# Sample tokens projected on the last prompt tile's mixer weights, with part of these weights kept in SBUF and a 4 KB descriptor ring

## The chip, the cores and the metric

The kernel runs on one core of one Trainium2 chip. The metric is the device time of one execution in microseconds (us), the median over runs. Lower is better. TensorE is called PE in the profile, VectorE DVE, ScalarE ACT, GpSimd POOL and SyncE SP; SP, ACT and POOL also issue DMAs.

## The reference

One layer of a decoder is computed for 512 prompt tokens (with 16 meta tokens ahead) and for 64 sample tokens (8 sequences of 8). All numbers are float32.

```python
D_MODEL = 1024; HP = 8; NK = 128; N_EXPERTS = NK * NK; DPK = 256; PEER_TOPK = 16
hp = hp + merge_heads(oa, ob, z, ...)          # ends in y @ w_out, w_out is [1024, 1024]
hp = hp + peer_ffn(rmsnorm(hp, norm2), peer_wq, peer_keys, peer_u, peer_v)

def peer_ffn block:                             # for each token
    q = (xb @ wq).reshape(-1, HP, 2, DPK // 2)
    s = einsum('thcd,hcnd->thcn', q, keys)      # scores against 2 x 128 keys for each head
    ...top 16 of each side, top 16 of the 256 sums -> 16 experts e for each of 8 heads
    h = einsum('td,thkd->thk', xb, u[e])
    w = softmax(sc) * gelu(h)
    return einsum('thk,thkd->td', w, v[e])
```

Before this come attention (group A, with a paged cache for the sample tokens) and a gated-delta recurrence (group B). Their outputs are concatenated to 1024 columns, projected by `w_out` and added to x. That projection is called the mixer in the kernel. The same steps are done for prompt and sample tokens, with the same weights. For each token 128 rows of u and v are then read (8 heads x 16 experts).

## The kernel before

The prompt is worked in 4 tiles of 128 tokens (`PT` = 4), and the 64 sample tokens are a fifth tile (`NT` = 5), which stands in 128 rows: each token twice, so that the two halves can choose experts of different heads. Its 128 experts per token then need 64 steps instead of 128.

**The gather loop.** A step is called a slot. There are 4 x 128 + 64 = 576 slots, and each one handles one expert for each of 128 rows. POOL issues an indirect DMA (L988) that gathers 128 rows of 2048 floats (u and v side by side, 8 KB) into one of `RING` = 8 buffers `uv`. DVE multiplies the u half with the normed tokens and sums (L1783), ACT makes the slot's weight (L1351, L1355) and a diagonal matrix of it (L1362), and PE multiplies the diagonal with the v half into PSUM banks 0 and 1 (L2194; four recorded matmuls of 128x512 for each slot). In some slots (`added_here`: two of five, in slots 33 to 49 and 72 to 104 of tiles 0 to 2, and in all of tile 3) DVE adds the v half to `hres` instead (L1757). A buffer is gathered into again when PE, or DVE, is done with it.

**The order of other work.** All other work of a tile is done between the slots of the tile before. Each engine's program is one queue; a step has a due time in slots (`route_at`, `att_at`, `choose_at` and so on), and `advance` puts it in front of the first slot that is due later. So the order on each engine is fixed by hand, and engines wait for each other by semaphores. For prompt tile n, with times in slots: the recurrence from 128(n-1)+11, attention from 128(n-1)+50, the mixer and routing from 128(n-1)+74 (`route_at(n, k)` is that plus 1.05 k), the choice of experts from 128(n-1)+101.

**The mixer.** `mix(n)` on PE transposes the tile's 128 x 1024 mixed heads into banks 4 and 5; ACT copies them to `rT` (`mix_copy`); PE multiplies them with the weights in four parts (two column halves of 512, each in two parts of 4 blocks of 128 rows; each part is 8 recorded matmuls, L2125). DVE adds x (`residual`, L1663) and the result lies in `hres`. Then come the transposes of `normed`, ACT's copies to `rT` (`normed_copy`), and four groups of routing queries and key scores (`queries`, L2161, L2171).

**The loads.** `route_loads(n)` on SP loads six things for each prompt tile: the two halves of the mixer weights (2048 KB each, into the two halves of `zone`) some 18 steps before `route_at(n, 0)`, then four parts of routing weights and keys (2304 KB each). For tile 3 parts 2 and 3 go to another place (`held`), parts 4 and 5 into `zone` over the mixer weights, when the matmuls of tile 3's mixer halves have read them. The routing weights of tile 3 stay for the sample tokens.

The sample tokens' mixer is different: `last_mixer_loads` loads the mixer weights again in four quarters of 1024 KB into one buffer in `Sw`, each when the one before has been used, and `mix(4)` multiplies them from slot 422 on, five slots apart (`last_mix_at`). x is loaded into `Sw` at slot 419, and the sum goes to half of `hres`.

**SBUF.** The compiler keeps 16 KB of each partition, from address 0, for the descriptors of DMAs that POOL issues. The kernel gives no size, so this default holds.

Of the kernel before, what the change touches and what calls it, by code (L numbers as in the profile page):

```python
# [16 lines left out]
D = 1024  # L17
# [65 lines left out]
NEVER = 1.0e9  # L83

# [153 lines left out]
def last_mix_at(c):  # L238
    return route_at(PT, 2) + 5 * c


# [6 lines left out]
def hybrid_step(nc: bass.Bass, i, o, stay_table, early_table, past_table):  # L248

    ctx = ExitStack()  # L250
    with ctx:
# [14 lines left out]
        stay = keep("stay", [128, NSTAY])  # L266
        minus_half = keep("minus_half", [128, 16])
# [66 lines left out]
        mix_part = G["Sw"][:, 2 * NPOS:2 * NPOS + 4 * HW]  # L334
# [255 lines left out]
        s_wrl = sem("last_mixer_weights_loaded")  # L590
        s_mxw = sem("last_mixer_weights_used")
# [55 lines left out]
        with nc.Block() as block:  # L647

            @block.sync
            def _(sp):  # L650
# [106 lines left out]
                def route_loads(n):  # L757
                    apart = n + 1 == PT
                    for part in range(6):
# [24 lines left out]
                def last_mixer_loads():  # L784
                    for c in range(4):
                        yield last_mix_at(c) - (8 if c == 0 else 4)
                        if c == 0:
                            sp.wait_ge(s_pv, NH * PT)
                        elif c % 2:
                            sp.wait_ge(s_mxw, c // 2 + 1)  # L790
                        else:
                            sp.wait_ge(s_yp, 2 * PT + 1)
                        cols = slice(4 * HW * (c % 2), 4 * HW * (c % 2) + 4 * HW)
                        sp.dma_start(mix_part, i["w_mixer"][c // 2][:, cols]).then_inc(s_wrl, 16)

                def residual_load(n):
                    yield route_at(n, -1)
                    if n < PT:
                        sp.wait_ge(s_wt, NH * (n + 1))
                        sp.dma_start(G["S"][:, 0, 0:D], i["x_prompt"][0, 128 * n:128 * n + 128, :]).then_inc(s_x2, 16)  # L800
                    else:
                        sp.wait_ge(s_wt, NH * PT)
                        sp.wait_ge(s_h2, 2 * PT)
                        for r in range(2):
                            sp.dma_start(G["S"][NSAMP * r:NSAMP * r + NSAMP, 0, 0:D], i["x_sample"].rearrange("b s d -> (b s) d")).then_inc(s_x2, 16)
# [39 lines left out]
                def store(t):  # L845
# [4 lines left out]
                    else:  # L850
                        sp.dma_start(o["y_sample"].rearrange("b s d -> (b s) d"), hres[0:NSAMP, t % 2, :]).then_inc(s_yst, 16)
# [4 lines left out]
                work += [Stream(route_loads(n)) for n in range(PT)] + [Stream(last_mixer_loads())] + [Stream(residual_load(n)) for n in range(NT)] + [Stream(past_biases())]  # L856
# [134 lines left out]
            def _(act):  # L991
# [285 lines left out]
                def mix_copy(n):  # L1277
                    yield route_at(n, 1)
                    for half in range(2):
# [5 lines left out]
                        rows = OUT_ROWS[n]  # L1285
                        for r0 in range(0, 128, rows):
                            ins = nc.scalar.activation(R["rT"][:, 4 * half:4 * half + 4, r0:r0 + rows], bank[4 + half][:, 0:4 * rows].rearrange("p (k r) -> p k r", k=4), ACT.Copy)  # L1287
                        ins.then_inc(s_mxc, 1)

                def residual_square(n):  # L1290
# [3 lines left out]
                    nc.scalar.activation(xn2[:, n % 2, :], hres[:, n % 2, :], ACT.Square, accum_out=G["ss2"][:, n:n + 1]).then_inc(s_ss, 1)  # L1294
# [46 lines left out]
                work += [Stream(mix_copy(n)) for n in range(NT)] + [Stream(residual_square(n)) for n in range(NT)] + [Stream(normed_copy(n)) for n in range(NT)]  # L1341
# [23 lines left out]
            def _(dve):  # L1365
# [288 lines left out]
                def residual(n):  # L1654
                    yield route_at(n, 8)
                    dve.wait_ge(s_x2, 16 * (n + 1) + 16 * (n == PT))
                    dve.wait_ge(s_mxp, 2 * (n + 1))
                    if n == PT:
                        dve.wait_ge(s_yst, 16 * (PT - 1))
                    for half in range(2):  # L1660
                        dve.wait_ge(s_yp, 2 * n + half + 1)
                        cols = slice(512 * half, 512 * half + 512)
                        nc.vector.tensor_tensor(hres[:, n % 2, cols], bank[6 + half][:, :], G["S"][:, 0, cols], ALU.add).then_inc(s_h2, 1)  # L1663
# [95 lines left out]
                def output(t):  # L1759
# [4 lines left out]
                    for half in range(2):  # L1764
                        cols = slice(512 * half, 512 * half + 512)
                        nc.vector.tensor_tensor(hres[0:rows, t % 2, cols], bank[half][0:rows, :], hres[0:rows, t % 2, cols], ALU.add).then_inc(s_yo, 1)
# [21 lines left out]
            def _(pe):  # L1788
# [312 lines left out]
                def mix(n):  # L2101
                    yield route_at(n, 0)
                    rows = OUT_ROWS[n]
                    pe.wait_ge(s_oa, 2 * (n + 2) if n < PT else 2)
                    pe.wait_ge(s_ob, 2 * (n + 2) if n < PT else 2)
                    if n:
                        pe.wait_ge(s_s2c, 4 * n)
                    for half in range(2):
                        for k in range(4):
                            r0 = NSAMP * (n == PT and half == 0)  # L2110
                            src = hres[:, n % 2, (4 * half + k) * 128:(4 * half + k + 1) * 128] if n < PT else obl[r0:r0 + rows, k * 128:(k + 1) * 128]
                            ins = nc.tensor.transpose(bank[4 + half][:, k * rows:(k + 1) * rows], src, stay[r0:r0 + rows, r0:r0 + rows])
# [133 lines left out]
```

## Time and profile before

| | |
|---|---|
| median of 3 runs | 2078.03 us (2075.93 to 2081.49) |
| profiled execution, first to last instruction | 2073.5 us |
| PE busy | 1706.2 us, 82% |
| DVE busy | 1336.6 us, 64% |
| ACT busy | 801.7 us, 39% |
| POOL busy | 765.6 us, 37% |
| DMA moved | 770.18 MB, 371 GB/s over the span |
| gathers (L988) | 576, 1188 ns of POOL each on average |

The span leaves out what lies around the first and the last instruction, and one profiled execution is not the median of the runs; 2078.03 - 2073.5 = 4.5 us is the difference here. Busy time of PE is modelled: a matmul that waits for its weights counts as busy. PEld are PE's weight loads, beside the matmuls. The line of slices cuts the span into 40 equal pieces of 51.8 us, and each digit is a share in tenths. The DMA share is the mean over the core's 16 DMA engines. A DMA's landing time runs from its issue to its last byte's arrival, so it includes the time that it stood in line. A wait is put down to what ended it last.

### The profile page before, as it was taken

What the parts mean: (1) busy time and instruction counts of PE and PEld (TensorE: products, weight loads), DVE (VectorE), ACT (ScalarE), POOL (GpSimd) and SP (SyncE); (2) the same over time, 40 slices, a digit from 0 to 9 for tenths busy, and PEclk for the clock granted to TensorE, in tenths of its full rate; (3) what the DMA queues carried; (4) which work ended last, traced back from release to release, by engine and by line L of the source; (5) the groups of instructions that cost most, each with busy time, mean ns of one, the idle gap of its engine ahead of it and who ended that gap; (6) DMA issues with size and microseconds to landing.
All of it is one profiled execution on the core that took longest, in us unless ns stands there. A gap on an engine that the chain in (4) does not pass through costs nothing.

```text
span 2073.5 us, 20564 instructions
## 1 busy us (share of the span) xinstructions
PE 1706.2 (82%) x6211; PEld 858.6 (41%) x6211; DVE 1336.6 (64%) x3023; ACT 801.7 (39%) x2371; POOL 765.6 (37%) x670
## 2 busy tenths in 40 slices
PE   7697999988997978889787888978797677866777
PEld 2242465547453444445344535433463223532211
DVE  1344514345897667887655888864688866679544
ACT  1342322222545433463533445453344423333432
POOL 2111110111444442436344343634444444554442
PEclk9799999999999999999898899988998888998999
DMA  9999723138999999999999999999999999999997
GB/s 336 346 311 388 256 77 117 46 117 331 405 417 424 428 426 427 426 425 420 423 417 426 427 426 397 419 423 386 426 427 409 427 427 427 427 427 427 427 427 315
DMA packets 137447, 770.18 MB, mean 371 GB/s; under 512 B 15311, under 2 KB 24287, under 8 KB 60008
## 3 DMA queue, kind: packets, MB, share of 16 engines
q0 software_dynamic: 88448, 622.22, 72.3%
q1 hardware_dynamic: 45408, 139.34, 17.8%
q10 hardware_dynamic: 3480, 7.31, 0.9%
q8 instruction: 49, 0.80, 0.1%
q14 instruction: 62, 0.51, 0.1%
HBM read 752.83 MB, written 16.26 MB: 371 GB/s over the span
## 4 chain that ended last, share of the span: by engine, by line
PE 35%; DMA 34%; DVE 16%; ACT 7%; issue 4%; POOL 2%; SPq 1%; ACTq 0%; DVEq 0%; POOLq 0%
DMA sb_uv<-in_peer_uv,sb_eidx 29%; PE bank L2194 15%; PE bank L1804 7%; DVE sb_uv L1783 7%; PE bank L2125 2%; PE bank L2161 2%; DVE sb_hres L1757 2%; DMA sb_hres<-pre_conv 1%; POOL sb_uv L988 1%; ACT sb_diag L1362 1%; DMA sb_zone<-in_w_route 1%; PE bank L1918 1%; DMA sb_Sw<-in_w_mixer 1%; PE bank L1930 1%; ACT sb_ew L1355 1%
## 5 line engine op out<-in xcount | busy, mean ns | idle before, releaser
L2194 PE MATMUL bank<-sb_uv,sb_diag 128*128 128x512 f32 (+1 forms) x1860 | 949.4, 647 | 271.9 <-ACT sb_diag L1362 262.1
L988 POOL DMA_INDIRECT sb_uv<-in_peer_uv,sb_eidx x576 | 684.3, 1188 | 875.1 <-PE bank L2194 662.8
L1783 DVE CUSTOM_DVE_ANT_0 sb_uv<-sb_uv,sb_xn 128x1024 f32<-128x1024 f32 x576 | 699.7, 1221 | 319.9 <-DMA sb_uv<-in_peer_uv,sb_eidx 317.4
L2194 PEld LDWEIGHTS bank<-sb_uv,sb_diag 128*128 128x128 f32 (+1 forms) x1860 | 335.7, 195 | 764.0 <-ACT sb_diag L1362 436.9
L1351 ACT ACTIVATE sb_gel<-sb_h 128x1 f32<-128x1 f32 x576 | 116.3, 202 | 778.9 <-DVE sb_h L1783 776.1
L1804 PE MATMUL bank<-sb_w,sb_xnT 128*128 128x512 f32 (+1 forms) x560 | 264.6, 615 | 24.4 <-DMA sb_w<-in_w_sections 11.5
L1362 ACT ACTIVATE sb_diag<-sb_stay,sb_ew 128x128 f32<-128x128 f32 (+1 forms) x465 | 183.2, 394 | 48.0 <-PE bank L2194 4.8
L1355 ACT ACTIVATE sb_ew<-sb_gel,sb_gate 128x1 f32<-128x1 f32 x576 | 169.7, 295 | 19.9
L1804 PEld LDWEIGHTS bank<-sb_w,sb_xnT 128*128 128x128 f32 (+1 forms) x560 | 98.6, 187 | 146.2 <-issue 121.8
L1757 DVE SCALAR_TENSOR_TENSOR sb_hres<-sb_uv,sb_ew,sb_hres 128x1024 f32<-128x1024 f32 x111 | 142.3, 1282 | 0.0
L2161 PEld LDWEIGHTS bank<-sb_rT,sb_zone 128*128 128x128 f32 x1024 | 122.4, 193 | 20.9 <-issue 20.6
L2161 PE MATMUL bank<-sb_rT,sb_zone 128*128 128x128 f32 x1024 | 123.8, 276 | 1.9 <-issue 1.8
L2125 PE MATMUL bank<-sb_zone,sb_rT 128*128 128x512 f32 x128 | 59.4, 612 | 7.4 <-ACT sb_rT L1287 7.4
L912 POOL TENSOR_TENSOR sb_rstd<-sb_ms,sb_minus_half 128x8 f32<-128x8 f32 (+1 forms) x10 | 16.4, 1640 | 112.2 <-DVE sb_ms L1466 112.2
L1783 DVE DVE_READ_ACCUMULATOR2_ANT sb_h<- 128x1 f32 x576 | 47.4, 82 | 0.0
L1351 ACT ACT_TABLE_LOAD x33 | 42.3, 1283 | 0.6
L2125 PEld LDWEIGHTS bank<-sb_zone,sb_rT 128*128 128x128 f32 x128 | 25.0, 197 | 39.4 <-issue 39.4
L1688 DVE FIND_INDEX8 sb_tix<-sb_top,sb_score 128x8 uint32<-128x128 f32 x144 | 38.4, 285 | 0.0
L1684 DVE MAX8 sb_top<-sb_score 128x8 f32<-128x128 f32 x144 | 31.4, 279 | 7.0 <-ACT sb_score L1323 6.9
L2161 PEld LDWEIGHTS bank<-sb_rT,sb_held 128*128 128x128 f32 x256 | 32.2, 199 | 6.8 <-issue 6.8
L1530 DVE TENSOR_TENSOR sb_X<-sb_X,bank 128x256 f32<-128x256 f32 (+1 forms) x36 | 14.7, 408 | 30.4 <-PE bank L1930 28.8
L2125 PE MATMUL bank<-sb_Sw,sb_rT 128*128 128x512 f32 x32 | 23.4, 900 | 11.0 <-DMA sb_Sw<-in_w_mixer 10.3
(341 smaller groups left out, 1566.5 us busy)
## 6 DMA issues: line engine op xcount, KB each, us to landing
sb_zone<-in_w_route SPq DMA_DIRECT2D x14, 2304.0 KB, 11.8
sb_w<-in_w_sections SPq DMA_DIRECT2D x40, 512.0 KB, 7.1
sb_zone<-in_w_mixer SPq DMA_DIRECT2D x8, 2048.0 KB, 15.5
sb_uv<-in_peer_uv,sb_eidx POOLq DMA_INDIRECT x576, 14.4
sb_sS<-in_cache_kT SPq DMA_DIRECT2D x32, 256.0 KB, 7.6
sb_zone<-in_cache_kT SPq DMA_DIRECT2D x32, 256.0 KB, 7.3
sb_held<-in_cache_v SPq DMA_DIRECT2D x32, 256.0 KB, 7.4
sb_zone<-in_cache_v SPq DMA_DIRECT2D x32, 256.0 KB, 5.7
```

The lines of the kernel that those rows point to most:

```text
L988: nc.gpsimd.indirect_dma_start(uv[:, m % RING, :], None, i["peer_uv"], bass.IndirectOffsetOnAxis(ap=eidx[:, t % 2, n:n + 1], axis=0)).then ...
L1351: nc.scalar.activation(G["gel"][:, at], G["h"][:, at], ACT.Gelu).then_inc(s_dg, 1)
L1355: nc.scalar.activation(G["ew"][:, at], G["gel"][:, at], ACT.Copy, scale=gate[:, t % 2, n:n + 1]).then_inc(s_dg, 1)
L1362: nc.scalar.activation(G["diag"][:, d % DIAGS, 0:cols], eye, ACT.Copy, scale=G["ew"][:, at]).then_inc(s_dg, 1)
L1684: n_top = count.inc(nc.vector.max(top[:, q, k:k + 8], sets[q]), s_tk)
L1688: n_used = count.inc(nc.vector.max_index(tix[:, q, k:k + 8], top[:, q, k:k + 8], sets[q]), s_cut if k and q == quads[-1] else s_tk)
L1757: nc.vector.scalar_tensor_tensor(hres[:, t % 2, :], uv[:, m % RING, D:2 * D], G["ew"][:, m % 8:m % 8 + 1], hres[:, t % 2, :], ALU.mult, AL ...
L1783: nc.vector.tensor_tensor_reduce(out=uv[:, m % RING, 0:D], in0=uv[:, m % RING, 0:D], in1=xn2[:, t % 2, :], scale=1.0, scalar=0.0, op0=ALU. ...
L1804: ins = nc.tensor.matmul(bank[b][0:rows, :], lhsT=xT(t)[:, kk, :], rhs=F["w"][:, piece % PIECES, kk % 2, :], start=kk == 0, stop=kk == KC - 1)
L2125: ins = nc.tensor.matmul(bank[6 + half][:, :], lhsT=R["rT"][:, 4 * part + k, :], rhs=weights[:, k, :], start=part + k == 0, stop=part == 1 ...
L2161: ins = nc.tensor.matmul(bank[6 + j % 2][:, 128 * s:128 * s + 128], lhsT=weights_part(n, g + 2)[:, k, 128 * s:128 * s + 128], rhs=R["rT"][ ...
L2194: ins = nc.tensor.matmul(bank[half][0:rows, :], lhsT=G["diag"][:, d % DIAGS, 0:rows], rhs=uv[:, m % RING, D + 512 * half:D + 512 * half + ...
```

## The change

Three things are changed.

1. `DMA_RING` = 4096: the descriptor ring of POOL's DMAs is given as 4 KB per partition instead of the default of 16 KB. The 12 KB go to a new buffer `mix_kept` of 6 blocks of 128 x 512 floats (`KEPT` = 6 of the 16 blocks of the mixer weights, three eighths).
2. The six blocks are loaded once, for tile 0, by a DMA of their own. For every tile the first half's load brings only blocks 6 and 7. `mixer_row` picks the kept block or the loaded one. The second half is loaded in full for each prompt tile, as before.
3. `last_mixer_loads` and `last_mix_at` are gone. The sample tokens are projected in `sample_mix`, on PE right behind the mixer of tile 3, with tile 3's weights in `zone` and `mix_kept`. Their transposes come at `route_at(3, 2.5)`, ACT copies them (`sample_mix_copy`) to the part of `zone` behind the weights, and the four parts of matmuls come at `route_at(3, 8)` to 12.5, into banks 2 and 3. x is loaded twice (for both halves of the rows) into `samp_x` in `Sw`, behind tile 3's x; DVE adds there at `route_at(3, 16.5)`, and the end result is also formed there and stored from there. The loads of routing parts 4 and 5 of tile 3 go over the mixer weights, so they now wait for all four parts of the sample projection (`s_yp` at 10).

The steps of the sample tile after that (`normed(4)`, `queries(4, g)`, the choices) keep their due times.

```diff
@@ constants
+KEPT = 6
+DMA_RING = 4096
-def last_mix_at(c):
-    return route_at(PT, 2) + 5 * c
@@ hybrid_step
+        mix_kept = keep("mix_kept", [128, KEPT, HW])
-        mix_part = G["Sw"][:, 2 * NPOS:2 * NPOS + 4 * HW]
+        samp_x = G["Sw"][:, 2 * NPOS:2 * NPOS + D]
+        samp_mT = [R["zone"][:, half, KC * HW:ZONE].rearrange("p (k r) -> p k r", k=4) for half in range(2)]
+        def mixer_row(n, half, k):
+
+            return mix_kept[:, k, :] if half == 0 and k < KEPT else weights_part(n, half)[:, k, :]
@@ route_loads (SP)
-                            sp.wait_ge(s_yp, 2 * n + part - 3)
+                            sp.wait_ge(s_yp, 2 * (PT + 1))
...
-                            sp.dma_start(weights_part(n, part), i["w_mixer"][part].rearrange("p (k n) -> p k n", k=KC)).then_inc(s_wr[part % 2], 16)
+                            first = KEPT * (part == 0)
+                            weights = i["w_mixer"][part].rearrange("p (k n) -> p k n", k=KC)
+                            if n == 0 and part == 0:
+                                sp.dma_start(mix_kept[:, :, :], weights[:, 0:KEPT, :]).then_inc(s_kept, 16)
+                            sp.dma_start(weights_part(n, part)[:, first:, :], weights[:, first:, :]).then_inc(s_wr[part % 2], 16)
...
-                def last_mixer_loads():
-                    for c in range(4):
-                        yield last_mix_at(c) - (8 if c == 0 else 4)
...
-                        sp.dma_start(mix_part, i["w_mixer"][c // 2][:, cols]).then_inc(s_wrl, 16)
@@ residual_load (SP)
+                    sp.wait_ge(s_wt, NH * (n + 1))
+                    sp.dma_start(G["S"][:, 0, 0:D], i["x_prompt"][0, 128 * n:128 * n + 128, :]).then_inc(s_x2, 16)
+                    if n + 1 == PT:
                         for r in range(2):
-                            sp.dma_start(G["S"][NSAMP * r:NSAMP * r + NSAMP, 0, 0:D], i["x_sample"].rearrange("b s d -> (b s) d")).then_inc(s_x2, 16)
+                            sp.dma_start(samp_x[NSAMP * r:NSAMP * r + NSAMP, :], i["x_sample"].rearrange("b s d -> (b s) d")).then_inc(s_xs, 16)
@@ ACT
+                def sample_mix_copy():
+                    yield route_at(PT - 1, 2.6)
+                    for half in range(2):
+                        act.wait_ge(s_mxp, 2 * PT + half + 1)
+                        for r0 in range(0, 128, NSAMP):
+                            ins = nc.scalar.activation(samp_mT[half][:, :, r0:r0 + NSAMP], bank[4 + half][:, 0:4 * NSAMP].rearrange("p (k r) -> p k r", k=4), ACT.Copy)
+                        ins.then_inc(s_mxc, 1)
@@ residual (DVE)
+                    else:
+                        yield route_at(PT - 1, 16.5)
+                        dve.wait_ge(s_xs, 32)
...
+                            nc.vector.tensor_tensor(samp_x[:, cols], bank[2 + half][:, :], samp_x[:, cols], ALU.add).then_inc(s_h2, 1)
@@ mix (PE)
+                                ins = nc.tensor.matmul(bank[6 + half][:, :], lhsT=R["rT"][:, k, :], rhs=mixer_row(n, half, k), start=k == 0, stop=k == KC - 1)
...
+                def sample_mix():
+                    yield route_at(PT - 1, 2.5)
+                    pe.wait_ge(s_mxc, 2 * PT)
+                    for half in range(2):
+                        for k in range(4):
+                            r0 = NSAMP * (half == 0)
+                            ins = nc.tensor.transpose(bank[4 + half][:, k * NSAMP:(k + 1) * NSAMP], obl[r0:r0 + NSAMP, k * 128:(k + 1) * 128], stay[r0:r0 + NSAMP, r0:r0 + NSAMP])
+                        ins.then_inc(s_mxp, 1)
+                    for half in range(2):
+                        for part in range(2):
+                            yield route_at(PT - 1, 8 + 3 * half + 1.5 * part)
...
+                                ins = nc.tensor.matmul(bank[2 + half][:, :], lhsT=samp_mT[k // 4][:, k % 4, :], rhs=mixer_row(PT - 1, half, k), start=k == 0, stop=k == KC - 1)
+                        ins.then_inc(s_yp, 1)
@@ kernel
-    nc = bacc.Bacc("TRN2", target_bir_lowering=False, num_devices=1)
+    nc = bacc.Bacc("TRN2", target_bir_lowering=False, num_devices=1, dynamic_dma_scratch_size=DMA_RING)
```

## Rows read from the trace of the kernel before

**Rows 1.** The page: 40 slices, busy tenths of DMA and GB/s moved.

```profile
DMA  9999723138999999999999999999999999999997
GB/s 336 346 311 388 256 77 117 46 117 331 405 417 424 428 426 427 426 425 420 423 417 426 427 426 397 419 423 386 426 427 409 427 427 427 427 427 427 427 427 315
```

**Rows 2.** Stretches of 40 us over the whole run; the first line names the columns.

```profile
core 0: us, PE busy (x) PEld busy (x) DVE busy (x) ACT busy (x) POOL busy (x), PEclk, DMA share, GB/s
1260.00:1300.00 40.00, 37.23 (x151) 21.43 (x150) 34.15 (x75) 20.63 (x61) 17.27 (x15) 1.00 1.00 387
1380.00:1420.00 40.00, 32.13 (x99) 16.23 (x100) 22.70 (x43) 22.79 (x66) 16.43 (x15) 0.93 0.90 367
1700.00:1740.00 40.00, 28.58 (x60) 11.68 (x58) 25.18 (x38) 11.51 (x42) 19.65 (x16) 0.87 1.01 427
1940.00:1980.00 40.00, 31.42 (x66) 7.45 (x64) 19.73 (x32) 14.15 (x51) 16.14 (x16) 1.00 1.01 427
```

**Rows 3.** The DMA view of the whole run: total, and the gathers' queue.

```profile
DMA packets 137447, 770.18 MB, mean 371 GB/s; under 512 B 15311, under 2 KB 24287, under 8 KB 60008
...
q0 software_dynamic: 88448, 622.22, 72.3%
```

**Rows 4.** The page, DMA issues of the mixer weights: count, KB each, us to landing.

```profile
sb_zone<-in_w_mixer SPq DMA_DIRECT2D x8, 2048.0 KB, 15.5
...
sb_Sw<-in_w_mixer SPq DMA_DIRECT2D x4, 1024.0 KB, 8.9
```

**Rows 5.** Gathers (L988), whole run: POOL's wait for PE, and issue to landing.

```profile
  PE bank L2194: 662.8, 371
...
DMA to landing us min/median/max: 5.4/14.4/24.4
```

**Rows 6.** The chain that ended last, near the end: start, length, what.

```profile
1987.36 15.11 DMA sb_uv<-in_peer_uv,sb_eidx
```

**Rows 7.** Gathers issued between 1390 and 1400 us, in attention of tile 3.

```profile
L988 POOL DMA_INDIRECT sb_uv<-in_peer_uv,sb_eidx x2: 947/1294/1640, 1390.8 to 1395.3; - x2
...
DMA to landing us min/median/max: 6.2/7.3/8.3
```

**Rows 8.** Two short stretches, columns as in rows 2.

```profile
1360.00:1370.00 10.00, 4.65 (x13) 2.06 (x12) 5.29 (x10) 3.37 (x9) 1.89 (x2) 0.83 1.00 425
1400.00:1405.00 5.00, 5.00 (x16) 2.41 (x15) 2.48 (x6) 3.00 (x11) 2.92 (x2) 0.92 0.27 79
```

**Rows 9.** Gathers issued between 1440 and 1460 us, in tile 3's mixer.

```profile
L988 POOL DMA_INDIRECT sb_uv<-in_peer_uv,sb_eidx x7: 933/938/1732, 1441.8 to 1459.4; - x7
...
DMA to landing us min/median/max: 18.3/20.1/23.5
```

**Rows 10.** The mixer's matmuls (L2125), whole run: ns min/median/max, first and last start.

```profile
L2125 PE MATMUL bank<-sb_zone,sb_rT x128: 592/592/1194, 456.0 to 1454.6; 128*128 128x512 f32 x128
...
L2125 PE MATMUL bank<-sb_Sw,sb_rT x32: 592/1060/1223, 1675.5 to 1725.2; 128*128 128x512 f32 x32
...
  DMA sb_Sw<-in_w_mixer: 23.1, 6
```

**Rows 11.** PE in order of time around tile 3's mixer: start, length, what, idle before.

```profile
1441.34 3.60 PE L2125 MATMUL bank<-sb_zone,sb_rT 128*128 128x512 f32 x8
1444.78 1.88 PE L2194 MATMUL bank<-sb_uv,sb_diag 128*128 128x512 f32 x4
1446.49 3.60 PE L2125 MATMUL bank<-sb_zone,sb_rT 128*128 128x512 f32 x8
...
1472.09 3.78 PE L2194 MATMUL bank<-sb_uv,sb_diag 128*128 128x512 f32 x4 [7.51 <-ACT sb_diag L1362]
```

**Rows 12.** Tile 3's route loads (L782), 1400 to 1470 us: issue, and issue to landing.

```profile
L782 SPq DMA_DIRECT2D sb_zone<-in_w_route x2: 327/328/328, 1445.0 to 1455.3; - x2
...
DMA to landing us min/median/max: 11.7/12.8/23.0
```

**Rows 13.** Queries that read zone, 1520 to 1530 us: count, busy, mean.

```profile
L2161 PE MATMUL bank<-sb_rT,sb_zone 128*128 128x128 f32 x29 | 3.6, 275 | 0.0
```

More of the change, by code:

```diff
@@ L1293, in residual_square @@
                     act.wait_ge(s_ass, NH * min(n + 2, NT))
-                    nc.scalar.activation(xn2[:, n % 2, :], hres[:, n % 2, :], ACT.Square, accum_out=G["ss2"][:, n:n + 1]).then_inc(s_ss, 1)
+                    if n == PT:
+                        act.wait_ge(s_yo, 2 * (PT - 1))
+                    nc.scalar.activation(xn2[:, n % 2, :], hres[:, n % 2, :] if n < PT else samp_x, ACT.Square, accum_out=G["ss2"][:, n:n + 1]).then_inc(s_ss, 1)
                 def normed_copy(n):
@@ L1765, in output @@
                         cols = slice(512 * half, 512 * half + 512)
-                        nc.vector.tensor_tensor(hres[0:rows, t % 2, cols], bank[half][0:rows, :], hres[0:rows, t % 2, cols], ALU.add).then_inc(s_yo, 1)
+                        out = hres[:, t % 2, cols] if t < PT else samp_x[0:rows, cols]
+                        nc.vector.tensor_tensor(out, bank[half][0:rows, :], out, ALU.add).then_inc(s_yo, 1)
                 work = [Stream(xT_gains())] + [Stream(x_mean(n)) for n in range(NT)] + [Stream(gates())] + [Stream(conv(m)) for m in range(3 * NT)] + [Stream(qk_norm(u)) for u in range(2 * NT)]
@@ L2109, in mix @@
                         for k in range(4):
-                            r0 = NSAMP * (n == PT and half == 0)
-                            src = hres[:, n % 2, (4 * half + k) * 128:(4 * half + k + 1) * 128] if n < PT else obl[r0:r0 + rows, k * 128:(k + 1) * 128]
-                            ins = nc.tensor.transpose(bank[4 + half][:, k * rows:(k + 1) * rows], src, stay[r0:r0 + rows, r0:r0 + rows])
+                            ins = nc.tensor.transpose(bank[4 + half][:, k * 128:(k + 1) * 128], hres[:, n % 2, (4 * half + k) * 128:(4 * half + k + 1) * 128], st("ident"))
                         ins.then_inc(s_mxp, 1)
@@ L2123, in mix @@
-                            weights = weights_part(n, half)[:, 4 * part:4 * part + 4, :] if n < PT else mix_part.rearrange("p (k n) -> p k n", k=4)
-                            for k in range(4):
-                                ins = nc.tensor.matmul(bank[6 + half][:, :], lhsT=R["rT"][:, 4 * part + k, :], rhs=weights[:, k, :], start=part + k == 0, stop=part == 1 and k == 3)
-                            if n == PT and part == 0:
-                                ins.then_inc(s_mxw, 1)
+                                pe.wait_ge(s_mxc, 2 * (n + 1))
@@ L2135, in normed @@
                             kk = 4 * half + k
-                            ins = nc.tensor.transpose(bank[4 + half][:, k * 128:(k + 1) * 128], hres[:, n % 2, kk * 128:(kk + 1) * 128], st("ident"))
+                            src = hres[:, n % 2, kk * 128:(kk + 1) * 128] if n < PT else samp_x[:, kk * 128:(kk + 1) * 128]
+                            ins = nc.tensor.transpose(bank[4 + half][:, k * 128:(k + 1) * 128], src, st("ident"))
                         ins.then_inc(s_xnT_ps, 1)
@@ L2176, in _ @@
                 work += [Stream(attention_head(n, h)) for n in range(PT) for h in range(NH)] + [Stream(past(p)) for p in range(NPAIR)]
-                work += [Stream(mix(n)) for n in range(NT)] + [Stream(normed(n)) for n in range(NT)] + [Stream(turned_back(n)) for n in range(NT)] + [Stream(queries(n, g)) for n in range(NT) for g in range(4)]
+                work += [Stream(mix(n)) for n in range(PT)] + [Stream(sample_mix())] + [Stream(normed(n)) for n in range(NT)] + [Stream(turned_back(n)) for n in range(NT)] + [Stream(queries(n, g)) for n in range(NT) for g in range(4)]
                 advance(work, -200)
```

65 lines of the change are left out of this document (29 added, 36 removed).

## The prediction

> **What bounds the kernel now.** I read the page's slices first. From slice 11 on (518 us) the DMA line is all nines, nearly always at 405 to 428 GB/s, and only the last slice falls [rows 1]. Next I read the table of stretches. At 1700 and at 1940 us the DMA share is 1.01 at 427 GB/s and PE is busy 28.6 and 31.4 us of 40; two stretches fall short, 1260 to 1300 (387 GB/s, PE 37.2 of 40) and 1380 to 1420 (share 0.90) [rows 2]. Then the queues: the gathers' queue moved 622 MB of 770 MB [rows 3]. One gather is 128 rows of 8 KB, 1.049 MB, so 1.049/427 = 2.456 us of DMA time. The gathers took 14.4 us (median) from issue to landing, that is 14.4/2.456 = 5.9 gathers' worth of queue, and POOL waited 662.8 us for PE to free one of the eight buffers [rows 5]. That wait is no sign that PE is late: eight buffers turn in 8 x 2.456 = 19.6 us whatever PE does, and the chain near the end shows just such turns, 15.11 us of DMA in each [rows 6]. From landing to the next issue of the same buffer there are 19.6 - 15.1 = 4.5 us of engine work. So from about 510 us to the last gather, bytes cost time, at 427 GB/s, as long as gathers are queued. The spare is seen in the landing time: once the gathers had begun, it fell to 6.2 us only where the DMA ran dry, between 1390 and 1405 us [rows 7, 8]. A landing time well above 6.2 us means a queue that can absorb a late engine.
>
> **Sum to be made against.** The profiled span is 2073.5 us; the median of the three runs, 2078.0, is 4.5 us above it. I carry the 4.5 over unchanged.
>
> **Bytes removed.** The mixer weights come as 8 loads of 2048 KB (two for each prompt tile) and 4 of 1024 KB for the sample tokens [rows 4].
> - Kept blocks: 6 of the 8 blocks of the first half, 0.75 x 2.097 = 1.573 MB, are no longer loaded for tiles 1 to 3: 4.72 MB, 11.05 us at 427 GB/s.
> - Sample tokens: 4 x 1.049 = 4.19 MB go, 9.8 us. Their weights were used from 1675.5 to 1725.2 us and loaded shortly before, where the DMA was full [rows 2, 10].
> - Tile 0's weights are loaded before the gathers, the same bytes in one DMA more: no time, since the DMA was far from full there (slice 9, 415 to 467 us, 117 GB/s) [rows 1]. Without that cover it would be one SP issue, 0.33 us by a route load's [rows 12]. The two loads of the sample tokens' x move from before the last tile's end to before tile 3's mixer, with the same bytes.
> Together 8.91 MB, 20.9 us, if the DMA stays full.
>
> **PE, the moved projection.** The 32 sample matmuls and 8 transposes move from the stretch after 1670 us to right behind tile 3's mixer, about 1457 us. They took 0.59 to 1.22 us each as recorded, by the granted clock,, and PE stood 23.1 us in all waiting for their weights (both PE rows together) [rows 10]; that wait goes, but the DMA was full all the time, so it gives nothing by itself. At full clock eight take 3.44 us and a gather's four 1.71 us, together 5.15 us (starts at 1441.34, 1444.78 and 1446.49) [rows 11]. In this stretch DVE takes two of five gathers, so a part with a step of 1.575 slots costs PE 3.44 + 0.6 x 1.575 x 1.71 = 5.06 us, against 1.575 x 2.456 = 3.87 us of DMA. PE falls back 1.2 us per part, or 1.6 if a part comes with somewhat more of the gathers' work, so 4.8 to 6.4 us in four parts, and about 1 us more for the eight transposes and the ACT copies that now stand ahead of gathers' work on ACT. Behind these on PE are tile 3's transposes, its queries and every gather's use; POOL waits for the latter. Is there spare? Gathers issued in 1440 to 1460 landed after 20.1 us [rows 9], but 5.5 to 11 us of that are the two route loads of 2304 KB (2.36 MB, 5.5 us each), issued at 1445.0 and 1455.3 [rows 12], which the change holds back until the sample projection is done. What is left, 9 to 14.6 us, less 6.2, is a spare of 2.8 to 8.4 us against a lag of 5.8 to 7.4. So the DMA runs dry for nothing up to 4.6 us; if one part ran at the lower of PE's clocks, where the longest of these matmuls took 1.19 us instead of 0.59 [rows 10], 3.4 us more, up to 8. I take 2 us, nearer to the low end, as the lag of tile 3's own mixer was absorbed there in the same way without a gap.
>
> **The route loads held back.** SP waits for all ten counts of the projection, and part 5 and nothing else due soon is queued behind it. They would be issued near 1480 instead of 1445 and 1455. The slowest such load landed after 23.0 us [rows 12], so by about 1503; they are first read at about 1520 [rows 13]. Cost nothing; if gathers crowd them further, PE stands, and the eight buffers cover some 8 us.
>
> **ACT and DVE.** The four ACT copies, the two DVE additions and the squares are the same work at another place. They cost nothing while the gathers are queued. The sample tokens now read and write their own buffer instead of a half of hres, which removes a wait on a store that ended long before.
>
> **Where saved bytes may not pay.** Between 1260 and 1300 PE is nearly full and the rate falls to 387 GB/s [rows 2], and in 1390 to 1405 attention's steps through PE, ACT and DVE do: a gap of 0.73 x 5 = 3.65 us [rows 8]. A shorter load of mixer weights just before (6.1 us of DMA instead of 9.8) gives the engines 3.7 us less to catch up in. But PE was busy only 4.65 of 10 us in 1360 to 1370 [rows 8], so it had more time than it needed. The loss lies between 0 and 3.7 us for tile 3, with less for tiles 1 and 2; I take 1 us.
>
> **The ring.** The trace of before has no row for descriptor room. Gathers in flight are 5.9 on average and at most 8, so the old ring had room for at least 8. A quarter of that is at least 2. The queue held 88448 packets for 576 gathers and some smaller DMAs, so under 153.6 packets a gather, 9.6 for each of 16 DMA engines [rows 3]. Bounds: a small gain (a shorter list to look through; POOL's 0.947 us an issue is hidden anyway, so zero) to the rival below. I take zero.
> The Trainium skill, DMA: Bandwidth & Descriptors, The descriptor swizzle and Terms, gives 9 read and 9 write descriptors of 16 bytes per engine for a 1 MiB transfer; an estimate from that page is 4096/144 = 28 gathers in the smaller ring against 8 in flight, so by it the sum stays. The trace's packet count agrees with the 9.
>
> **Sum.** 2073.5 - 20.9 + 2 + 1 = 2055.6; + 4.5 = 2060.1. I say 2060.
>
> **Rivals.**
> 1. *PE starves the DMA at the doubled mixer.* The lag eats the whole spare and the lower clock comes in: 8 to 12 us lost, 2078.0 - 20.9 + 10 = 2067. For it: the held loads no longer cover PE. Against: PE stood idle 7.51 us before 1472.09, soon after tile 3's mixer, for late gathers [rows 11]. 13%.
> 2. *The engines set the pace of tiles 1 to 3.* Then their 11.05 us only widen gaps like that of 1400, and the sample tokens' 9.8 us alone pay: 2068.2. For it: 387 GB/s and 3.65 us of gap in rows 2 and 8. Against: a DMA share of 1.0 elsewhere. 7%.
> 3. *Slower: the ring holds POOL back.* If the smaller ring leaves room for only two gathers in flight, the pace is 6.2/2 = 3.1 us instead of 2.456, so 576 x 0.64 = +371 us and 2428 us. It decides from below 6.2/2.456 = 2.5 gathers in flight; less drastic forms (a stop at each turn of the ring) cost less but pass the 20.9 us soon. For it: only the bound of 2. Against: the packet count. 6%.
> 4. *It does not do what it says,* with bytes saved but taken back by small losses in all places, within 0.3%: 2072 to 2084, middle 2078. 4%.
> The forecast itself has 70%, and its own range is 2056 to 2064.
>
> **Chances and range.** A measurement of this kernel can tell about 0.3%, 6.2 us, from no change. Faster: the forecast, rival 1 and nearly all of rival 2, 88%; the same 5%; slower 7%. Range: the full 20.9 us without loss gives 2057.1, less 2.6 for the spread of the runs is 2054.5; above, rivals 1 and 2 up to 2070.
>
> **What would show it.** The issues view: eight w_mixer loads cut to small ones for the first half, none into Sw; total near 761 MB. The stretches from 600 to 2020 still at 427 GB/s and a share of 1.0; a gap near 1460 to 1480 would be rival 1, one wider than 3.65 us near 1400 rival 2; landing times of gathers pinned low with POOL waiting for neither PE nor DVE would be the ring. PE's wait for Sw weights near 1690 is gone. Wrong would be the whole, if the landing time showed spare everywhere and the time still did not fall.

## The result, and the profile after

| | before | changed |
|---|---|---|
| median of 4 runs, same series | 2076.98 us (2075.77 to 2081.49) | 2054.43 us (2052.61 to 2061.15) |
| ratio | | 0.989, 95% interval 0.9871 to 0.9909 |
| profiled execution, first to last instruction | 2073.5 us | 2050.8 us |
| DMA moved | 770.18 MB | 761.27 MB |
| POOL's wait for PE before gathers | 662.8 us | 642.7 us |

The changed kernel is 22.6 us faster between the medians, 22.7 us between the profiled spans. In a second series of its own (the first experiment below) it measured 2060.01 us. The forecast of 2060.0 is 5.6 us above the first median, and 2054.43 lies 0.07 us under the low end. The median of all eight runs of the changed kernel is 2058.0 us. Each of its two profiles, of 2050.8 and 2052.0 us, is of the quickest execution in its series: the eight spans go up to 2059.5 us, with a median of 2056.2. The profile of before, 2073.5 us, is of a quick execution too. What is read from these profiles below holds for such executions.

The page of the changed kernel: the slices, the total and the gathers' queue [rows 1, 3].

```profile
DMA  9999723127999999999999999999999999999997
GB/s 346 344 309 374 264 96 118 47 103 305 399 427 401 426 427 428 426 426 416 427 420 426 427 426 394 414 425 411 417 427 426 415 427 427 427 426 427 427 427 321
...
DMA packets 137015, 761.27 MB, mean 371 GB/s; under 512 B 15263, under 2 KB 24239, under 8 KB 60472
...
q0 software_dynamic: 88448, 622.22, 73.2%
```

The line of tenths has not changed in kind: all nines from slice 11 to slice 39. The kernel is bound as before, and the bytes have gone: 770.18 - 761.27 = 8.91 MB, what the prediction counted. The gathers' queue holds the same 622.22 MB in the same 88448 packets, so the smaller ring changed nothing in how gathers are cut.

The issues view of the changed kernel, the loads of mixer weights (count, KB each, median us to landing) [rows 4].

```profile
sb_zone<-in_w_mixer SPq DMA_DIRECT2D x4, 2048.0 KB, 13.9
...
sb_zone<-in_w_mixer SPq DMA_DIRECT2D x4, 512.0 KB, 8.0
...
sb_mix_kept<-in_w_mixer SPq DMA_DIRECT2D x1, 1536.0 KB, 6.6
```

The second halves still come whole, the first halves as 512 KB, the kept blocks once, and nothing goes to `Sw`.

Gathers (L981 now) over the whole run, and the chain near the end [rows 5, 6].

```profile
  PE bank L2217: 642.7, 378
...
DMA to landing us min/median/max: 5.7/13.7/26.8
```
```profile
1945.03 15.11 DMA sb_uv<-in_peer_uv,sb_eidx
```

The turn of the eight buffers still holds 15.11 us of DMA. The queue is nearly as full as before: 13.7/2.456 = 5.6 gathers' worth, after 5.9.

Stretches of the changed kernel, columns as in [rows 2, 8]. The short ones lie around the attention of tile 3 (1360 to 1415) and around the projection of the sample tokens (1455 to 1465).

```profile
1260.00:1300.00 40.00, 37.36 (x162) 22.55 (x161) 33.42 (x72) 21.66 (x64) 18.08 (x15) 1.00 0.99 383
1360.00:1370.00 10.00, 6.74 (x24) 3.17 (x21) 7.20 (x12) 5.39 (x14) 2.37 (x2) 1.00 1.00 426
1380.00:1400.00 20.00, 17.46 (x59) 9.10 (x58) 9.21 (x20) 12.24 (x40) 9.14 (x8) 1.00 1.01 424
1400.00:1405.00 5.00, 2.45 (x5) 0.87 (x4) 3.55 (x6) 1.79 (x6) 2.90 (x2) 0.87 0.98 418
...
1410.00:1415.00 5.00, 3.63 (x14) 1.61 (x12) 1.23 (x2) 0.90 (x3) 1.75 (x2) 1.00 1.06 304
...
1455.00:1460.00 5.00, 5.00 (x13) 2.22 (x12) 5.00 (x9) 1.60 (x6) 4.11 (x3) 1.00 0.99 388
1460.00:1465.00 5.00, 5.00 (x13) 2.15 (x12) 3.27 (x5) 2.09 (x7) 2.35 (x2) 1.00 0.98 380
...
1700.00:1740.00 40.00, 29.11 (x104) 15.58 (x103) 27.82 (x42) 15.07 (x52) 21.20 (x18) 0.87 1.01 427
1940.00:1980.00 40.00, 31.28 (x65) 7.63 (x66) 19.96 (x33) 13.82 (x49) 17.80 (x17) 1.00 1.01 427
```

The gap of 1400 (share 0.27 before) is not there in this execution, nor some us earlier, where the same work now lies (424 GB/s from 1380 to 1400). Between 1455 and 1465 the rate dips to 388 and 380 GB/s, 5 x (1 - 388/427) + 5 x (1 - 380/427) = 1.0 us of DMA time. By the share it is 5 x 0.01 + 5 x 0.02 = 0.15 us, so the queue did not run dry. From 1425 to 1500 us the bytes moved fall 1.2 us short of 427 GB/s, against 0.0 before, so no more than this is lost near the projection in this execution. The long stretches stand as before: 427 GB/s at 1700 and at 1940, and 383 GB/s at 1260, where PE is nearly full. From 1360 to 1370 PE is busier than it was at that time (6.74 us of 10 instead of 4.65), and the DMA share is still 1.00. The work of PE around the moved projection, in order of time (L2126 is the prompt tile's mixer, L2145 the sample tokens' projection, L2159 its transposes) [rows 11]:

```profile
1441.82 1.88 PE L2217 MATMUL bank<-sb_uv,sb_diag 128*128 128x512 f32 x4
1443.54 3.60 PE L2145 MATMUL bank<-sb_mix_kept,sb_zone 128*128 128x512 f32 x8
1446.97 1.88 PE L2217 MATMUL bank<-sb_uv,sb_diag 128*128 128x512 f32 x4
1448.69 1.04 PE L2159 MATMUL bank<-sb_stay,sb_hres 128*128 128x128 f32 x8
...
1454.71 3.60 PE L2145 MATMUL bank<-sb_zone 128*128 128x512 f32 x8
1458.15 1.88 PE L2217 MATMUL bank<-sb_uv,sb_diag 128*128 128x512 f32 x4
1459.87 3.60 PE L2145 MATMUL bank<-sb_zone 128*128 128x512 f32 x8
1463.30 1.88 PE L2217 MATMUL bank<-sb_uv,sb_diag 128*128 128x512 f32 x4
...
1487.36 2.93 PE L2217 MATMUL bank<-sb_uv,sb_diag 128*128 128x512 f32 x3 [6.03 <-ACT sb_diag L1362]
```

The last part starts 5.16 us after the third (1454.71, 1459.87), with one gather's four matmuls between them, and PE has no idle time until 1475. While it falls behind, the landing time of the gathers falls towards 6.2 us; it recovers behind. Gathers issued 1450 to 1460, then 1460 to 1470 [rows 9]:

```profile
DMA to landing us min/median/max: 7.3/8.6/10.9
```
```profile
DMA to landing us min/median/max: 11.6/17.9/19.5
```

The route loads that were held back (L790), with their landing [rows 12]:

```profile
L790 SPq DMA_DIRECT2D sb_zone<-in_w_route x2: 333/466/599, 1463.5 to 1463.9; - x2
...
DMA to landing us min/median/max: 13.5/17.2/21.0
```

They were issued as soon as the last sample part had ended (1459.87 + 3.60 = 1463.47). From then on PE can catch up, and before 1487.36 it is PE that waits, 6.03 us.

### The profile page after: what moved, and what is told of

The parts are those of the page before. It is cut to its first block, busy times and chain, and to the rows that moved or that the text cites. A ratio compares the mean times of both kernels' runs of the same rounds, so it can differ in the third digit from the quotient of the medians.

```text
span 2050.8 us, 20558 instructions
## 1 busy us (share of the span) xinstructions
PE 1701.6 (83%) x6211; PEld 856.9 (42%) x6211; DVE 1334.9 (65%) x3023; ACT 801.3 (39%) x2371; POOL 788.8 (38%) x670
## 2 busy tenths in 40 slices
DMA packets 137015, 761.27 MB, mean 371 GB/s; under 512 B 15263, under 2 KB 24239, under 8 KB 60472
## 3 DMA queue, kind: packets, MB, share of 16 engines
q0 software_dynamic: 88448, 622.22, 73.2%
## 4 chain that ended last, share of the span: by engine, by line
PE 38%; DMA 29%; DVE 15%; ACT 6%; issue 5%; SPq 4%; POOL 2%; ACTq 0%; DVEq 0%; POOLq 0%
DMA sb_uv<-in_peer_uv,sb_eidx 26%; PE bank L2217 17%; DVE sb_uv L1789 7%; PE bank L1810 7%; PE bank L2184 3%; PE bank L2126 2%; POOL sb_uv L981 1%; DVE sb_hres L1762 1%; SPq L816 1%; SPq L820 1%; ACT sb_diag L1362 1%; ACT sb_ew L1355 1%; SPq L832 1%; DMA sb_zone<-in_w_route 1%; SPq L836 1%
## 5 line engine op out<-in xcount | busy, mean ns | idle before, releaser
L981 POOL DMA_INDIRECT sb_uv<-in_peer_uv,sb_eidx x576 | 707.5, 1228 | 835.1 <-PE bank L2217 642.7
L2126 PE MATMUL bank<-sb_zone,sb_rT 128*128 128x512 f32 x80 | 36.0, 592 | 0.0
L1530 DVE TENSOR_TENSOR sb_X<-sb_X,bank 128x256 f32<-128x256 f32 (+1 forms) x36 | 14.7, 408 | 30.4 <-PE bank L1936 28.8
L1438 DVE TENSOR_TENSOR sb_xin<-sb_xin,sb_taps 128x2048 f32<-128x2048 f32 (+1 forms) x8 | 18.3, 2288 | 22.0 <-DMA sb_xin<-pre_conv 22.0
L2184 PE MATMUL bank<-sb_rT,sb_held 128*128 128x128 f32 x256 | 31.2, 275 | 0.0
## 6 DMA issues: line engine op xcount, KB each, us to landing
sb_uv<-in_peer_uv,sb_eidx POOLq DMA_INDIRECT x576, 13.7
```

Source lines behind the costliest of these rows:

```text
L981: nc.gpsimd.indirect_dma_start(uv[:, m % RING, :], None, i["peer_uv"], bass.IndirectOffsetOnAxis(ap=eidx[:, t % 2, n:n + 1], axis=0)).then ...
L2126: ins = nc.tensor.matmul(bank[6 + half][:, :], lhsT=R["rT"][:, k, :], rhs=mixer_row(n, half, k), start=k == 0, stop=k == KC - 1)
L2184: ins = nc.tensor.matmul(bank[6 + j % 2][:, 128 * s:128 * s + 128], lhsT=weights_part(n, g + 2)[:, k, 128 * s:128 * s + 128], rhs=R["rT"][ ...
```

## The experiments

My theory: from the first gather to the last, a byte costs 1/427 us per KB, whatever it is read for, and PE's lag at the doubled mixer is covered by the queue. The rivals were that only a part of the bytes pays (rival 2), that the ring costs something (rival 3), and that PE starves the DMA at 1460 (rival 1). Ratios are to the kernel before in the same series, which had a median of 2079.6 us beside experiments 1 to 4 (20 runs of it) and of 2078.5 us beside experiments 5 to 8 (16 runs). Beside each ratio stands its 95% interval.

**1. The changed kernel again.** No edit.

> The changed kernel once more, in the same rounds as its parts. Both theories: 0.989 of the kernel before, 20.9 us or a little more. If the bytes theory holds (8.93 MB at 427 GB/s, gaps of the DMA equal in sum within 3 us), the gap of tile 3's attention near 1400 us may or may not come back, since it is worth at most 4 us; landing times of gathers fall to 7 or 8 us near 1455 us, behind the doubled mixer.

Measured: 2060.01 us (2053.8 to 2061.31), ratio 0.9908 (0.9889 to 0.9928). The gain is 19.6 us instead of 22.6, and one kernel's runs lie between 2052.6 and 2061.3 us over both series. The span of its profiled execution was 2052.0 us, close to the first.

**2. The ring alone.** The kernel before, with

```diff
-     nc = bacc.Bacc("TRN2", target_bir_lowering=False, num_devices=1)
+     nc = bacc.Bacc("TRN2", target_bir_lowering=False, num_devices=1, dynamic_dma_scratch_size=4096)
```

> The kernel before with the ring of 4096 bytes and nothing else. Bytes theory: same time, within 3 us of before, all 770 MB at 427 GB/s. Rival, the smaller ring helps (1.8 us or more of the 22.7 are its own): 2 us or more faster and POOL's issues shorter. Rival, the ring holds POOL back: slower, with landing times pinned low.

Measured: 2076.69 us (2069.97 to 2083.04, 10 runs), ratio 0.9989 (0.9974 to 1.0004), that is -2.3 us with -5.4 to +0.8. A cost of more than 0.8 us is excluded, and rival 3 with its 350 us all the more. A small gain is not excluded by the time, but POOL's issues of gathers did not become shorter: 1204 ns on average in its profile, 1188 before.

**3. The projection moved, nothing kept, the ring as before.** The changed kernel with `KEPT = 0`, no `mix_kept` and no size for the ring:

```diff
- KEPT = 6
+ KEPT = 0
...
-             return mix_kept[:, k, :] if half == 0 and k < KEPT else weights_part(n, half)[:, k, :]
+             return weights_part(n, half)[:, k, :]
```

> The changed kernel with no block kept and the default ring: only the sample projection moved, four loads of 1024 KB fewer (4.19 MB). Bytes theory: 9.8 us faster than before. If the double mixer on PE starves the DMA: less than 7 us faster. If the moved work also took something off PE that mattered: over 12 us faster.

Measured: 2070.06 us (2062.96 to 2078.3, 10 runs), ratio 0.9957 (0.9938 to 0.9976), that is -8.9 us (-12.9 to -5.0) where its 4.19 MB are worth 9.8. The interval holds the price of the bytes, but is too wide to exclude a loss or a gain of 3 us beside it. In its profile the DMA lost 1.7 us between 1450 and 1500 us, measured against 427 GB/s.

**4. Blocks kept, the projection where it was.** The kernel before with the ring of 4 KB and

```diff
+             mix_kept = keep("mix_kept", [128, KEPT, HW])
...
-                             sp.dma_start(weights_part(n, part), i["w_mixer"][part].rearrange("p (k n) -> p k n", k=KC)).then_inc(s_wr[part % 2], 16)
+                             first = KEPT * (part == 0)
+                             weights = i["w_mixer"][part].rearrange("p (k n) -> p k n", k=KC)
+                             if n == 0 and part == 0:
+                                 sp.dma_start(mix_kept[:, :, :], weights[:, 0:KEPT, :]).then_inc(s_kept, 16)
+                             sp.dma_start(weights_part(n, part)[:, first:, :], weights[:, first:, :]).then_inc(s_wr[part % 2], 16)
```

> The kernel before with the ring of 4096 bytes and six kept blocks, the sample tokens' weights still loaded again in four quarters. 4.72 MB fewer. Bytes theory: 11.1 us faster than before. Rival 2 (the engines set the pace of tiles 1 to 3, so the shorter loads only widen gaps): 0 to 4 us faster, and a gap of up to 7 us near 1400.

Measured: 2068.55 us (2062.4 to 2070.11, 5 runs), ratio 0.9942 (0.9922 to 0.9962), that is -12.1 us (-16.2 to -7.9) where its 4.72 MB are worth 11.05. Rival 2 gave these bytes nothing; the interval excludes that. The two parts together make -21.0 us, between the -19.6 and the -22.6 of the whole: they add up, within intervals of 4 us to each side. The totals of the DMA view, experiment 3 and then experiment 4, show that each took out its own bytes (770.18 - 765.99 = 4.19, 770.18 - 765.46 = 4.72):

```profile
DMA packets 136871, 765.99 MB, mean 371 GB/s; under 512 B 15247, under 2 KB 24223, under 8 KB 59944
```
```profile
DMA packets 137591, 765.46 MB, mean 371 GB/s; under 512 B 15327, under 2 KB 24303, under 8 KB 60536
```

**5. Fewer loads still.** Does the same price hold further on? The changed kernel, with only the last block of each half loaded for tiles 1 to 3. The weights of the other blocks are left out there, and their matmuls multiply by kept blocks instead:

```diff
-             return mix_kept[:, k, :] if half == 0 and k < KEPT else weights_part(n, half)[:, k, :]
+             return mix_kept[:, k % KEPT, :] if (half == 0 and k < KEPT) or (n and k < KC - 1) else weights_part(n, half)[:, k, :]
...
-                             first = KEPT * (part == 0)
+                             first = KEPT * (part == 0) if n == 0 else KC - 1
```

> The changed kernel with only block 7 of each half loaded for tiles 1 to 3; the other blocks' matmuls read kept blocks in their place, so the mixer of tiles 1 to 3 and of the sample tokens multiplies by the wrong weights. 2.10 MB fewer for each of three tiles, 6.29 MB. Bytes theory: 14.7 us faster than the changed kernel, 35.6 us faster than before (0.983). If the engines set the pace once the loads give them no time to catch up: 5 to 10 us faster than the changed kernel, with gaps of the DMA in tiles 0 and 2.

Measured: 2047.09 us (2039.68 to 2048.79), ratio 0.985 (0.982 to 0.988). The total of its DMA view:

```profile
DMA packets 137016, 754.98 MB, mean 370 GB/s; under 512 B 15264, under 2 KB 24240, under 8 KB 60857
```

Another 6.29 MB went, 14.7 us at 427 GB/s. By ratios the time fell 12 us from experiment 1 (0.9908 - 0.985, of 2078.5), or 8.3 us from the first series (0.989), and by profiled spans 2050.8 - 2037.9 = 12.9 us. In the profile the bytes account for it: from the first gather on, the DMA lost 34.8 us against 427 GB/s, 1.8 more than the 33.0 of the changed kernel, and 14.7 - 1.8 = 12.9. Intervals of 4 and 6 us to each side don't tell the time from the whole price, nor from the 5 to 10 us of the other theory, but they tell it from no gain at all, which rival 2 would give these bytes.

**6. One block more in each of two places, in a ring of 2 KB.** Seven blocks of the first half and one of the second are kept (`KEPT = (7, 1)`, the two loads of the kept blocks follow it), with

```diff
- KEPT = 6
- DMA_RING = 4096
+ KEPT = (7, 1)
+ DMA_RING = 2048
```

> The changed kernel with a ring of 2048 bytes and eight kept blocks (seven of the first half, one of the second). 2 x 0.262 MB fewer for each of tiles 1 to 3 than in the changed kernel, 1.57 MB. Bytes theory: 3.7 us faster than the changed kernel, 24.6 us faster than before. Ring theory (POOL is held back once fewer gathers fit): slower than the changed kernel, from a room of under 2.5 gathers on.

Measured: 2059.27 us (2052.5 to 2065.01), ratio 0.9902 (0.9875 to 0.993). That can't be told from the changed kernel (0.989, 0.9908), nor from 3.7 us below it. The profiled span was 2062.7 us, and it shows two places where the saving went in that execution. The gap at tile 3's attention was back (DMA share 0.53 from 1395 to 1400 us and 0.78 to 1405, 3.5 us), and from 600 to 640 us the rate was 360 GB/s, where the changed kernel had 395: 6.3 us lost instead of 3.0. From the first gather on it lost 43.0 us against 427 GB/s, 10 more than the changed kernel.

**7. A ring of 1 KB.** The changed kernel with

```diff
- DMA_RING = 4096
+ DMA_RING = 1024
```

> The changed kernel with a ring of 1024 bytes, a quarter of its own. If the ring has room for 28 gathers at 4096 bytes, 7 fit here, against the eight buffers: in flight are 5.9 on average, so the time stays within 0.3% of the changed kernel, with landing times above some 16 us cut off at most. If room was near its limit at 4096 already: slower by 3% or more.

Measured: 2062.13 us (2061.41 to 2063.75), ratio 0.992 (0.9889 to 0.995). Against 0.9908 that is 2.5 us more, with intervals of about 4 and 6 us to each side: no effect that the runs can tell. The landing of its gathers over the whole run:

```profile
DMA to landing us min/median/max: 5.6/13.7/25.8
```

No cut at 16 us shows, as the longest took 25.8. The median is the same 13.7 us as with 4 KB, and POOL waited 654.9 us for PE (642.7 with 4 KB). Had the ring held gathers back throughout, fewer would have stood in line, the landing time would have fallen and POOL would have waited for something else. A small cost is not excluded: this profile lost 39.0 us of DMA time from the first gather on, against 33.0 and 32.3 in the two profiles of the changed kernel, and experiment 6 lost 43.0. Most of the difference lies in places that vary from profile to profile (7.8 us at tile 3's attention here), and one profile for each ring can't tell the ring from this. By the 9 descriptors of 16 bytes that the Trainium skill, DMA: Bandwidth & Descriptors, The descriptor swizzle and Terms, gives per engine for a 1 MiB transfer, an estimate is 1024/144 = 7 gathers in such a ring, one fewer than the buffers; with 5.6 in line as a rule, the trace agrees that this costs little or nothing.

**8. How much spare PE had at the doubled mixer.** The changed kernel, with the 32 sample matmuls done twice into the same sum, which doubles the sample tokens' projection:

```diff
-                                 ins = nc.tensor.matmul(bank[2 + half][:, :], lhsT=samp_mT[k // 4][:, k % 4, :], rhs=mixer_row(PT - 1, half, k), start=k == 0, stop=k == KC - 1)
+                                 ins = nc.tensor.matmul(bank[2 + half][:, :], lhsT=samp_mT[k // 4][:, k % 4, :], rhs=mixer_row(PT - 1, half, k), start=k == 0, stop=False)
+                             for k in range(4 * part, 4 * part + 4):
+                                 ins = nc.tensor.matmul(bank[2 + half][:, :], lhsT=samp_mT[k // 4][:, k % 4, :], rhs=mixer_row(PT - 1, half, k), start=False, stop=k == KC - 1)
```

> The changed kernel with each of the 32 sample matmuls done twice into the same sum (the sample tokens' projection comes out doubled): 13.8 us more PE work at full clock, right behind tile 3's mixer, no byte more. If the spare there was used up in the changed kernel (landing times of 7 to 8 us against 6.2 when dry): 9 to 13 us slower than the changed kernel, with a gap of the DMA near 1460 us. If the queue still had 8 us of spare: 0 to 5 us slower.

Measured: 2068.34 us (2065.65 to 2074.75, 9 runs), ratio 0.9956 (0.9938 to 0.9973). By ratios this is (0.9956 - 0.9908) x 2078.5 = 10.0 us over the changed kernel in experiment 1, and 13.7 over its first series; the profiled spans differ by 2066.1 - 2050.8 = 15.3 us, of which some 4 us lie at tile 3's attention (6.2 us lost from 1360 to 1425, against 2.0). Its stretches, columns as before:

```profile
1455.00:1460.00 5.00, 5.00 (x19) 2.67 (x18) 0.00 (x0) 1.60 (x7) 0.94 (x1) 1.00 1.02 431
1460.00:1465.00 5.00, 5.00 (x13) 2.15 (x12) 3.37 (x5) 2.89 (x10) 0.00 (x0) 1.00 0.72 295
1465.00:1470.00 5.00, 5.00 (x13) 2.28 (x12) 5.00 (x10) 2.35 (x9) 2.38 (x2) 1.00 0.00 0
1470.00:1480.00 10.00, 10.00 (x24) 4.37 (x23) 2.25 (x3) 1.34 (x5) 3.59 (x4) 1.00 0.80 274
```

and what POOL waited for from 1455 to 1475 us (total, times, longest):

```profile
POOL sb_uv L981 <- PE bank L2219: 13.8, 2, 8.5
```

The DMA stood for 5 x 0.28 + 5 + 10 x 0.20 = 8.4 us, while PE was busy all the time and POOL waited for PE's use of a buffer. By bytes, 11.3 us were lost from 1425 to 1500, against 1.2 in the changed kernel. That is rival 1 as it was described, at 4 x 3.44 = 13.8 us more of matmuls. From 13.8 us of extra lag come 8.4 us of a dry DMA here (10 us in the time). So the changed kernel had some 4 to 5 us of spare left. By the landing time I would have said less: its lowest there is 7.3 us, 1.1 us above the 6.2 of a dry queue, and 6.8 us in experiment 1. The two don't agree closely, and the runs don't say why. Nor is 6.2 us a sharp edge: from 1260 to 1300 us of the kernel before, gathers landed after 7.8 to 11.1 us at 387 GB/s.

## Why the prediction came out as it did

**The bytes, and what they are worth.** Held. 8.91 MB went, 4.19 and 4.72 MB separately, and these parts measured -8.9 and -12.1 us for a forecast of 9.8 and 11.05.

**The sum.** The mechanism held, and the step that failed is a size: the +3 us of losses (2 at the doubled mixer, 1 at the attention), with 0.9 us from the offset. Forecast 2055.6 us for the span, measured 2050.8: 4.8 us less. To see where they are, I took for both kernels the time from the first gather to the end, less the bytes moved in it at 427 GB/s: 34.5 us of lost DMA time before, 33.0 in the changed kernel, 32.3 in its second profile. So in these executions the losses did not grow by 3 us, they fell by 1.5 to 2.2, and that is the difference of 4.8 but for rounding (3 + 1.5, and 0.2 from the first gather, 493.3 before and 493.1 now). All three are profiles of quick executions, but the medians say nearly the same: over all series it is 2079.1 us for the 40 runs of the kernel before and 2058.0 for the 8 of the changed one, a gain of 21.1 us, which is the 20.9 of the bytes and nothing taken off. Attention's 3.7 less and the mixer's 1.0 more make 2.7 less; the 1.2 that is missing was lost in several places, as between 600 and 640 us (395 GB/s, 412 before).
- *Doubled mixer, +2 us:* measured 1.0 us of dip. Landing times fell to 7.3 us and the share to 0.98: PE's lag ate into the spare, and by experiment 8 some 4 to 5 us of it were left. The bounds (0 to 4.6, up to 8) held it. Other profiles with the moved projection lost up to 1.9 us between 1450 and 1500 (experiment 7), so 2 us was a little high and no more. The lower clock that made the upper bound didn't come: all 32 sample matmuls took 592 to 595 ns with a granted clock of 1.00, the level of 2.4 GHz, as PE worked without a stop from before 1441 to 1475; before, they stood between idle times, with a granted clock of 0.81 on average from 1675 to 1726 us and a median of 1060 ns [rows 10].
- *Attention of tile 3, +1 us:* in this execution it was about -3.7. From 1360 to 1425 us the rate below 427 GB/s had cost 5.7 us before and cost 2.0 in the changed kernel, 1.4 of them from 1410 to 1415, where the sample tokens' x lands; before, this lay outside the stretch, at 1595. I had bounded it at "0 to 3.7" and allowed no gain. But the gap isn't a matter of the loads alone. Over the ten profiles of this study the same stretch lost between 1.8 us (experiment 4) and 7.8 us (experiment 7), and kernels that differ only in the ring's size stand at 2.0, 3.3 (the changed kernel, twice) and 7.8, and at 5.7 and 3.6 (before, and experiment 2). I can't say what brings the gap about in an execution, and the runs didn't test it. What they show is that the DMA time lost in this place alone differs by 6 us from profile to profile.
- *The offset, +4.5 us:* the unit was mis-sized. In each run of the changed kernel the time is some 1.8 us above its span (2052.61 and 2050.8, 2061.15 and 2059.4). The rest of the 4.5 us was where the profiled execution of before lay among its three runs; with the fourth run of the series it is 2076.98 - 2073.5 = 3.5 us. After the change the median lies 3.6 us above the profiled span, 0.9 less than I carried over.

**The low end of the range.** It came from the full 20.9 us, and 2.6 us more for the spread. Both were narrow: the bytes' gain isn't the largest possible (a gap can close as well), and the runs of the changed kernel spread by 8.7 us (2052.6 to 2061.3), so that the medians of two series differ by 5.6 us. The second series' 2060.01 lies on the forecast. That it does so is luck as much as the 0.07 us by which the first series lies under the range: both medians of four come from runs with that spread.

**The moved projection's timing.** The prediction had it at about 1457 us and the route loads near 1480. They came at 1443.5 to 1463.5 and at 1463.5. I had read the start off the trace of before, but by then 11.05 us of bytes are gone: the last matmul of the prompt tile's mixer started at 1454.6 before [rows 10] and starts at 1441.4 now. The spacing was right: 5.15 us forecast, 5.16 measured. The sum doesn't hang on the start.

**The route loads held back.** Nothing, as forecast: landed by 1463.9 + 21.0 = 1485 us, and what PE waited for before 1487.36 was a gather's diagonal from ACT, not a weight.

**The ring.** Zero, as forecast, within the interval of experiment 2 at 4 KB, and no effect that can be told at 2 KB and 1 KB, where a cost of some us stays possible.

**The sign of spare.** The prediction read the landing time as falling to 6.2 us only near 1400. It also fell to 5.4 us between 520 and 540 in the kernel before, where the rate was 348 GB/s from 520 to 530. The DMA fell short there too, so the sign stands, but 1400 was not its only place.

**The rivals.** Rival 1 has the right mechanism (experiment 8 shows it at 13.8 us more of PE work) and came into force with 1.0 us in the profile, at most 1.9 in any with the same matmuls, instead of 10. Rival 2 fell with experiments 4 and 5. Rival 3 with its 350 us fell with 2 and 7. Rival 4 fell with the result.

## What to carry to other kernels

Where the DMA is full from end to end, price a change by its bytes at the rate that the trace shows, and check it in parts: they added up here to within the measurement, some 4 us to each side. The landing time of the queued transfers is a rough gauge of spare: here 18 to 23 us was comfort and 7 to 9 us was near the edge, from which 13.8 us of lag cost 8.4 us of DMA. Look where the profiled execution lies among the runs before you add terms to its span. For the range take the spread of single runs and the gaps that come and go between executions, and let small losses have both signs.

## What the runs showed of the hardware that was not expected

- The descriptor ring can shrink from 16 KB to 4 and to 1 KB without a cost that 4 to 10 runs can tell (0.9989 for 4 KB alone, 0.992 against 0.9908 for 1 KB), at 8 KB rows and up to 8 gathers in flight. Only for 4 KB is a cost of a few us excluded. The freed SBUF held weights.
- A full DMA share isn't a full rate. From 1410 to 1415 us the changed kernel moved 304 GB/s at a share of 1.06, in the stretch where the two loads of the sample tokens' x (64 rows each) landed (issued 1394.8 and 1395.4, landing after 18.7 to 20.9 us); in the kernel before, where they landed at 1599.4 and 1602.5 us, it was 300 GB/s at 1.04 from 1595 to 1600. About 1.5 us in each kernel in these 5 us, moved with these loads. No run took them away, so that they cause it stays an inference. The stretch of the kernel before:

```profile
1595.00:1600.00 5.00, 3.51 (x4) 0.97 (x4) 3.53 (x6) 1.39 (x3) 2.61 (x2) 0.66 1.04 300
```

- The same matmul, 128x512 of float32, was recorded with 592 ns in a PE that was busy throughout, at a granted clock of 1.00, and with 1060 ns in the median (900 on average) where it stood between waits, at 0.81 on average. Its weight loads went along, 190 ns against 337 in the median. Work moved to a busy stretch became cheaper for PE by a third on average, as recorded:

```profile
L2145 PE MATMUL bank<-sb_zone x20: 592/592/593, 1451.3 to 1462.9; 128*128 128x512 f32 x20
```
